# A two-layer encoder: rows of negated mLSTM maxima spread over the partitions by transfers through memory instead of one-row matrix products

## What is computed

```python
def step(carry, inp):
    C, n, m_prev = carry
    qc, kc, vc, li, lf = inp
    b = jnp.cumsum(lf, axis=-1)
    logw = jnp.where(tril, b[..., :, None] - b[..., None, :] + li[..., None, :], NEG)
    inter = b + m_prev[..., None]
    m = jnp.maximum(jnp.max(logw, axis=-1), inter)
    a = jnp.exp(logw - m[..., None]) * jnp.einsum('bhtd,bhsd->bhts', qc, kc)
    ...
for l in range(DEPTH):
    ...
    x = x + jnp.concatenate([y_mla, y_dil, y_ml], axis=-1) @ w_out[l]
    x = x + hier_moe(rms_norm(x, norm_ffn[l]), ...)
```

## Time and profile before

| | |
|---|---|
| time, median of 3 runs | 1866.36 us (1862.82 to 1867.54) |
| time of the profiled execution | 1865.47 us |
| its span | 1863.5 us |
| PE busy | 1836.4 us, 99% |
| weight loads (PEld) busy | 1403.2 us, 75% |
| DVE busy | 739.9 us, 40% |
| ACT busy | 312.7 us, 17% |
| POOL busy | 8.5 us |
| HBM traffic | 291 GB/s over the span |

### The profile page before, as it was taken

One profiled execution on the slowest core, in us unless ns is written; L12 is line 12 of the kernel. 1 busy time (PEld: TensorE's weight loads), 2 busy tenths in 40 slices (PEclk: granted clock), 3 DMA queues, 4 the chain that ended last, 5 costly groups with the idle time before them and its releaser, 6 DMA issues.

```text
span 1863.5 us, 28400 instructions
## 1 busy us (share of the span) xinstructions
PE 1836.4 (99%) x12326; PEld 1403.2 (75%) x12326; DVE 739.9 (40%) x1545; ACT 312.7 (17%) x846; POOL 8.5 (0%) x17
## 2 busy tenths in 40 slices
PE   9999999999999999999899999999999999999998
PEld 8888887899775667666597888878987766667655
DVE  3567665577112122021236675655771122121112
ACT  3123122212101111011021131331121001111010
POOL 1000000000000000000000000000000000000000
PEclk9999999999999999999999999999999999999999
DMA  9433344347899999999964243352568999999995
GB/s 386 152 136 145 127 164 169 143 152 289 316 405 428 428 427 427 427 427 427 384 260 168 110 181 114 141 209 104 217 262 341 407 428 426 427 428 427 426 427 236
DMA packets 45551, 544.80 MB, mean 292 GB/s; under 512 B 5112, under 2 KB 5240, under 8 KB 12784
## 3 DMA queue, kind: packets, MB, share of 16 engines
q1 hardware_dynamic: 43632, 531.47, 69.6%
q0 software_dynamic: 1792, 11.46, 1.6%
HBM read 538.69 MB, written 4.22 MB: 291 GB/s over the span
## 4 chain that ended last, share of the span: by engine, by line
PE 97%; DVE 2%; issue 1%; DMA 0%; SPq 0%; ACT 0%; DVEq 0%
PE ps L787 94%; PE ps L841 1%; PE ps L1252 1%; PE ps L857 0%; PE ps L849 0%; DMA ring<-in_w_lat 0%; PE ps L1297 0%; DVE XN L1921 0%; DVE ring L1871 0%; PE ps L1155 0%; DVE v_mla L2040 0%; DVE scr L2009 0%; DVE ring L1816 0%; DVE ring L1806 0%; PE ps L1032 0%
## 5 line engine op out<-in xcount | busy, mean ns | idle before, releaser
L787 PE MATMUL ps<-ring,scr 128*64 128x256 f32 (+2 forms) x3488 | 628.3, 424 | 7.0 <-issue 7.0
L787 PEld LDWEIGHTS ps<-ring,scr 128*64 128x64 f32 (+1 forms) x3488 | 342.5, 138 | 213.4 <-issue 128.0
L787 PE MATMUL ps<-ring,XN 128*128 128x256 f32 (+2 forms) x1184 | 242.4, 361 | 1.2 <-DMA ring<-in_w_lat 1.2
L787 PEld LDWEIGHTS ps<-ring,XN 128*128 128x128 f32 x1184 | 210.7, 190 | 22.0 <-issue 2.6
L787 PE MATMUL ps<-ring,X 128*128 128x256 f32 x896 | 200.6, 379 | 0.0
L787 PE MATMUL ps<-XN,ring 128*128 128x128 f32 (+1 forms) x1312 | 196.2, 306 | 1.9 <-DVE X L1904 0.9
L787 PEld LDWEIGHTS ps<-XN,ring 128*128 128x128 f32 x1312 | 180.5, 192 | 15.0 <-issue 4.1
L787 PEld LDWEIGHTS ps<-ring,X 128*128 128x128 f32 x896 | 169.6, 190 | 22.7
L2082 DVE TENSOR_TENSOR v_mla<-scr,ps 128x256 f32<-128x256 f32 x32 | 13.5, 421 | 406.0 <-PE ps L787 406.0
L787 PE MATMUL ps<-PR,scr 128*64 128x256 f32 (+2 forms) x704 | 172.8, 402 | 0.0
L787 PE MATMUL ps<-BIAS,scr 128*64 128x256 f32 (+1 forms) x608 | 160.1, 421 | 4.6 <-issue 4.6
(11 more groups left out here) (274 smaller groups left out, 1471.9 us busy)
## 6 DMA issues: line engine op xcount, KB each, us to landing
ring<-in_moe_w_gate SPq DMA_DIRECT2D x46, 2048.0 KB, 22.0
ring<-in_moe_w_up SPq DMA_DIRECT2D x40, 2048.0 KB, 20.2
ring<-in_moe_w_down SPq DMA_DIRECT2D x38, 2048.0 KB, 24.7
ring<-in_w_main SPq DMA_DIRECT2D x36, 2048.0 KB, 9.5
ring<-in_w_out_a SPq DMA_DIRECT2D x16, 1280.0 KB, 6.8
PR<-in_moe_w_up SPq DMA_DIRECT2D x10, 2048.0 KB, 17.9
XN<-in_moe_w_down SPq DMA_DIRECT2D x10, 2048.0 KB, 20.8
BIAS<-in_moe_w_up SPq DMA_DIRECT2D x10, 2048.0 KB, 20.9
```

Source lines behind the costliest of these rows:

```text
L787: return pe.matmul(o, lhsT, rhs, start=start, stop=stop, skip_group_check=True)
```

## The change

`row_of_maxima` and its banks go. POOL stores `neg_m` (4 partitions, 8 KB) to memory once a layer, waits for that, waits for `ao3`, and reads the two rows of a head back with a source step of 0 over the 128 partitions, so that each partition gets 512 values (256 KB a transfer), into one of two buffers in `v_mla`. Heads 0 and 1 are read before the reload of `X`; heads 2 and 3 after it, each once ScalarE is done with the buffer (`decayed`). `masked` and `decays` read `maxima` instead of PSUM.

```diff
@@ plan_banks, plan_queries_keys: the banks of w0 to w3 are no longer planned
-                if h == 2:
-                    b.once("w3", 5)
...
-    if g == 0:
-        b.once("w0", 6)
-        b.once("w1", 7)
-    else:
-        b.once("w2", 5)
@@ tensors
+        maxima_dram = nc.dram_tensor("maxima_dram", (H_M, 2 * S), F32).ap()
+        maxima_out, maxima_in = sem("maxima_out"), [sem(f"maxima_in{b}") for b in range(2)]
+        maxima = vf[:, 0:4 * S].rearrange("p (b d s) -> p b d s", b=2, d=2)
@@ POOL
+                def load_maxima(h):
+                    pool.dma_start(maxima[:, h % 2, :, :].rearrange("p d s -> p (d s)"),
+                                   bass.AP(maxima_dram.tensor, h * 2 * S, [[0, P], [1, 2 * S]])).then_inc(maxima_in[h % 2], 16)
+                pool.wait_ge(*after("rows_ready", l, 1))
...
+                pool.dma_start(maxima_dram, neg_m[:, :, :].rearrange("h d s -> h (d s)")).then_inc(maxima_out, 16)
+                pool.wait_ge(maxima_out, 16 * (l + 1))
+                pool.wait_ge(*ready(f"ao{H_A // 2 - 1}", l))
+                load_maxima(0)
+                load_maxima(1)
                 pool.wait_ge(*ready(f"c12_{N_PAIR - 1}", l))
                 if l:
                     pool.wait_ge(x_out, 16 * l)
                 pool.dma_start(X[:, :, :], x_dram if l else a["x_t"]).then_inc(x_back, 16)
+                for h in range(2, H_M):
+                    pool.wait_ge(*after("decayed", l, h - 2))
+                    load_maxima(h)
@@ TensorE
-            def row_of_maxima(h, l):
-                name = f"w{h}"
-                pe.wait_ge(*freed(name, l))
-                for d in range(2):
-                    last = mm(bank(name)[:, d * S:(d + 1) * S], K[0:H_M, h:h + 1].to_broadcast([H_M, P]), grow(d, 0))
-                last.then_inc(*made(name))
...
                 queries_keys(0, l)
-                for h in range(2):
-                    row_of_maxima(h, l)
...
-                            if h in (1, 2):
-                                row_of_maxima(h + 1, l)
@@ VectorE, masked and weighted
-                    dve.wait_ge(*ready(f"w{h}", l))
+                    dve.wait_ge(maxima_in[h % 2], 16 * (H_M // 2 * l + h // 2 + 1))
...
-                            ins = dve.scalar_tensor_tensor(decay[:, h % 2, d, at:at + P], bank(f"w{h}")[:, d * S + t * P:d * S + (t + 1) * P],
+                            ins = dve.scalar_tensor_tensor(decay[:, h % 2, d, at:at + P], maxima[:, h % 2, d, t * P:(t + 1) * P],
...
-                    dve.wait_ge(*copied(f"w{h}", l))
+                    dve.wait_ge(*after("decayed", l, h))
@@ ScalarE, decays
-                        act.activation(decay[:, h % 2, d, at:at + P], bank(f"w{h}")[:, d * S + t * P:d * S + (t + 1) * P], ACT.Exp,
+                        act.activation(decay[:, h % 2, d, at:at + P], maxima[:, h % 2, d, t * P:(t + 1) * P], ACT.Exp,
...
-                    ins.then_inc(*read(f"w{h}"))
+                    ins.then_inc(*signal("decayed"))
```

More of the change, by code:

```diff
@@ L554, in build @@
                         ("gate_b", 1), ("gate_ln", 2), ("rows_ready", 2), ("em_ready", 1), ("uc_ready", 1),
-                        ("masked", H_M), ("r_ready", H_M), ("m_std", 1), ("o_gate", 1), ("y_ml", 1), ("w_rg", 1), ("sq2", N_OUT), ("acc2", N_OUT),
+                        ("masked", H_M), ("decayed", H_M), ("r_ready", H_M), ("m_std", 1), ("o_gate", 1), ("y_ml", 1), ("w_rg", 1), ("sq2", N_OUT), ("acc2", N_OUT),
                         ("ya_sums", 2), ("a1", N_APAIR), ("a2", N_APAIR), ("a3", N_APAIR), ("a4", N_APAIR),
@@ L776, in _ @@
                     pool.dma_start(BIAS[:, :, :], bass.AP(bias_dram.tensor, 0, [[1, P], [2 * S, H_D], [1, S + P]])).then_inc(bias_out, 16)
+                def load_maxima(h):
+                    pool.dma_start(maxima[:, h % 2, :, :].rearrange("p d s -> p (d s)"),
+                                   bass.AP(maxima_dram.tensor, h * 2 * S, [[0, P], [1, 2 * S]])).then_inc(maxima_in[h % 2], 16)
+                pool.wait_ge(*after("rows_ready", l, 1))
+                if l:
+                    pool.wait_ge(maxima_in[0], 16 * H_M // 2 * l)
+                    pool.wait_ge(maxima_in[1], 16 * H_M // 2 * l)
+                pool.dma_start(maxima_dram, neg_m[:, :, :].rearrange("h d s -> h (d s)")).then_inc(maxima_out, 16)
[3 more added lines that the diff above has]
+                load_maxima(1)
                 pool.wait_ge(*ready(f"c12_{N_PAIR - 1}", l))
```

## The result

The changed kernel takes 1855.12 us (median of 5 runs, 1850.75 to 1855.78) against 1866.94 us for the kernel before (5 runs). The ratio is 0.9936, with a 95% interval of 0.9925 to 0.9947: 11.9 us faster, between 9.9 and 14.0 (the medians differ by 11.8). The forecast was 1858.3 in a range of 1854.7 to 1861.8; the time lies inside it, 0.4 us above its fast edge. The profiled execution took 1855.24 us, its span is 1853.2 us, and it is 10.3 us shorter than the one of before. One later run of the kernel before, 1910.55 us, was in a slower state than all others and is in no mean here.

What follows compares the result with a forecast made beforehand. TensorE was taken to bound the kernel; 16 removed products at 4.03 us a layer give 8.06 us, added work costs nothing, so 1866.36 - 8.06 = 1858.3 us (chance 0.57), range 1854.7 to 1861.8.

Steps and rivals of the forecast that it cites:

- What bounds the kernel: Whole kernel: TensorE is 97% of the chain, so work taken from its list is worth its full length.
- The weight loads' share: TensorE: weight loads busy for 75% of the span, which by the Trainium skill's rule could mean something else bounds.
- The price of the removed products: TensorE, mLSTM: 16 float32 products priced from start to start, 4.03 us a layer, 8.06 us for both.
- The lower bound: Removed products at the rate of the queries' products ahead of head 2, 0.178 us a record: 5.7 us in all.
- rival 1: Layer 0's mLSTM: the half clock behind the removed products goes too, 1.7 us more gain, 1856.6 us; chance 0.23.
- VectorE and ScalarE at nothing: At `masked` and ScalarE's reads: on-chip reads cost nothing extra; without cover 8.6 us in all.
- The cover: VectorE behind `masked` for heads 0 and 1: 1.0 us to spare before the next addition's product arrives at 331.5.
- The transfers: POOL and DMA, five a layer: all land before `masked` asks; margin 108 us for heads 0 and 1, 16 for head 2.
- The gain passes through the experts: Experts: their load flood starts from TensorE's own point, so everything moves 4.03 us earlier and idle times stay.
- rival 2: Experts: transfers run from a fixed point and swallow the gain, 1866.4 us; partial form 1861; chance 0.13.
- The sign that I named: Profile after: layer 0's experts start 4 us earlier, layer 1's 8 us.
- Rival 3: At `masked(2)`: head 2's transfer lands late and TensorE runs out of banks; at 35 us, 1876 us; chance 0.03.

Runs made afterwards that it cites:

- the thin kernels: Kernels with products on 4 partitions, such as the changed kernel with all 16 put back unread: 1865.08 us, ratio 0.9993 to before.
- the filling: Changed kernel with spare products in TensorE's two idle times ahead of the experts: 1853.16 us; the same with 16 products on 4 partitions put back: 1863.43 us.
- the late transfer: Changed kernel with head 2's transfer held back until TensorE has finished queries_keys(1): 1862.50 us, ratio 0.9983 to before.

## Why the prediction was right, point by point

**What bounds the kernel**: right. TensorE is 97% of the chain before and after, and taken work was worth its length. The weight loads' share, 75% before and after, said nothing against it.

**The price of the removed products**: 4.03 us a layer from three starts; the stage shows 92.38 - 88.35 = 4.03 in the layer without a fall. The lower bound, 0.178 us a record from the queries' products, was not reached even by products on 128 partitions at the same places: 3.46 us a layer, 0.216 us a record. A thin one costs 0.252.

**The size of the whole**: the forecast of 8.06 us is 3.8 us short of the medians' difference, and the time is inside the range only because the range was drawn around rival 1. The term that was mis-sized is the clock's, which I put at nothing in the forecast and at 1.7 us in rival 1. By the mean clocks the change takes 4.5 us of toll away, worth 3.1 us. Rival 1 had the mechanism right for the part in the mLSTM, and its argument "it falls in one layer of two" against it was no argument: a fall there in one layer of two is 1.6 us a run on average in this kernel, and none without the group. Its time, 1856.6, is nearer to the measured 1855.1 than the forecast's is, though it had 0.23 and the forecast 0.57.

**VectorE and ScalarE at nothing**: right; 2.18 against 2.16 us for eight instructions. The cover was smaller than I reckoned, though: the addition behind them started at 330.09 without waiting, on a product that had ended at 327.48 + 2.50 = 329.98. I had taken its arrival from 333.45, which the half clock of that execution had made late. TensorE's next group covered the 0.1 us, and the next addition waits for TensorE again.

**The transfers**: hidden, with 19 us to spare instead of the 16 reckoned: 256 KB landed in 3.6 us, not 7, and VectorE came at 353.92 instead of 355.6, as the half-clock stretch is gone too. The run with the products back says the same: its stage is 92.37 us against 92.38 before, so the ten transfers cost nothing there.

**The gain passes through the experts**: right, and rival 2 falls. The experts' first load and the late starts moved by 4.3 to 4.5 us with the rest, though the DMA engines are full there. The better proof is that the stretch from the mLSTM's end to layer 1's queries takes the same 829.8 us in the three profiles without a fall in it, whether it starts at 410.4, 414.2 or 415.3. The sign that I named, layer 1's experts 8 us earlier, does not show as such in the first two profiles: its mLSTM ends 7.3 us earlier, for the different falls ahead of it.

**Rival 3**: its price was right in kind; the cover is 2.1 us (I had 2.5), and the 3 us beyond it were paid in full. Only one lateness was run.

**What stays open.** One fall behind the group of heads 0 and 1 a run is 1.7 of the 4.5 us of toll and costs 1.6 us. The others that the thin kernels have stand elsewhere, most often at the experts' start, 140 us behind that group, where TensorE is idle for 0.65 and 1.05 us in every kernel without the filling. Of the kernels without the filling, those with thin products have a fall there in 12 of 14 layers, those without in 3 of 10. Two of these three are the late transfer's, which has no thin product. Nothing shows how products could act on the clock 100 us later. Nor does the time at which the stage begins settle it: with 128 partitions and with the late transfer the two idle times end at the same moments of layer 0, 466.48 and 468.79, and the clock falls in the second alone. So some 1.5 us of the gain go with thin products by count, without a mechanism shown.

## What to carry to other kernels

Where TensorE's chain has no idle time, price a removed product by the starts of the groups around it, and look at the granted clock right behind it: a group of products on few partitions can cost the pace of what follows as well as its own time. A spread over partitions that is not needed soon can go by memory, here at no price that the runs show, as long as it is asked for later than it lands. Measure that margin: here the cover was 2.1 us, and of a wait of 5.1 us for the transfer TensorE paid 3.0. Compare mean granted clocks of several runs before reading a difference of 0.2% between two kernels, and don't count a half-clock stretch at half its length without looking where it fell: here 3.4 us at half the clock cost 1.6 us in the mLSTM and 0.7 to 0.8 late in the experts.

## What the runs showed of the hardware that was not expected

A fully busy TensorE can lose its clock: the granted clock fell from 1.00 to 0.50 behind groups of eight float32 records on 4 partitions by 256 columns (1.92 us) in 7 of 14 cases and behind a group of sixteen in 2 of 2, but not behind eight records on 128 partitions with other operands (two cases) nor behind groups of four. All other falls in the 14 profiles stand close behind 0.9 us or more of idle TensorE. A fall does not always cost half its length: of 1.7 us it cost 1.6 in the mLSTM, where TensorE had no idle time, and 0.7 to 0.8 late in the experts, where it had.

A thin product costs 0.72 us alone between others, 0.53 in groups of two and 0.48 in a group of four; one on 128 partitions in such groups 0.43. A read of the same 2 KB by 128 partitions (source step 0, 256 KB in all) landed in 3.4 to 3.7 us from POOL (medians of ten profiles), and in 5.4 us beside a load of weights; the store of 4 rows of 2 KB took 1.7 us.
